# A decoder layer's last FFN piece: its projection put behind the one before it, and its last four tiles multiplied for one half of the tokens at a time

## The chip, the cores and the metric

One core of one Trainium2 chip runs the whole layer in one launch. The metric is the device time of that launch in microseconds (us), and lower is better. Of several executions the median is given.

## The reference, cut to what matters

The kernel computes one decoder layer on 256 tokens of 2048 channels in float32: a token mixer, then a SwiGLU feed-forward network (FFN). Only the end of the FFN matters here.

```python
D_MODEL, SEQ, D_FF = 2048, 256, 5632

def rmsnorm(x, w):
    y = x * lax.rsqrt(jnp.mean(x * x, axis=-1, keepdims=True) + EPS)
    return y * w

def swiglu(h, w_gate_up, w_down):
    gate, up = jnp.split(h @ w_gate_up, 2, axis=-1)
    return (jax.nn.silu(gate) * up) @ w_down

# the last lines of the layer; x is (1, 256, 2048)
h = rmsnorm(x, g_pre_ffn) * (1.0 + sc_f) + sh_f
y = swiglu(h, w_gate_up, w_down)
x = x + ga_f * rmsnorm(y, g_post_ffn)
```

## The kernel before

**Tiles.** A weight tile is 256 rows by 512 columns of a matrix (512 KB). SyncE loads it into a ring of four slots (`RING = 4`), `raw`. ScalarE rounds it to `whi` (`high`), VectorE takes the rest, `raw - whi`, as `wlo` (`low`). TensorE multiplies it in `multiply`: for each half of the tokens (`tt`, 128 rows each) and each 128 rows of the tile three matmuls of 512 columns, so 12 per tile. The activations are split in the same way (`hT_hi` and `hT_lo` for the FFN's input, `oT_hi` and `oT_lo` for its hidden values). Each group of 512 output columns has a pair of PSUM banks, one bank for each half of the tokens. There are two such pairs, used in turn. Banks 4 and 5 (`XA`) take transposes.

**Who waits for whom.** `high(c)` waits until TensorE has finished tile c-4 (semaphore `multiplied`), `low(c)` waits for `high(c)`, TensorE waits for `low(c)` (`lo_ready`), and the load of tile c waits for `low(c-4)`. TensorE starts a group when its pair is free (`pair_free`). Each engine works through its own instructions in program order, and these are written out by hand: at which tile number `c` VectorE adds a finished pair or ScalarE takes a sigmoid stands in the loops over `c`.

**The FFN.** The 5632 hidden channels are 11 pieces of 512 (`NF = 11`, numbered 0 to 10 here). A piece has a gate (8 tiles), an up (8 tiles) and a projection back to 2048 columns (4 groups of 2 tiles). Between up and projection stands a chain: VectorE multiplies the SiLU of the gate by the up (`hidden`), TensorE transposes the product (`transpose_group`, 8 transposes), ScalarE rounds it (`hidden_high`, semaphore `ff_high`) and VectorE takes the rest (`hidden_low`, `ff_low`). To hide it, `channel(n)` runs on TensorE in the order gate of piece n, with the transposes of piece n-1 after its fourth tile, then projection of piece n-1, then up of piece n. VectorE adds the projection's pairs to `ya` with `add_pair`. Piece 10 is the loop `Fori(FF_ADA + 2, NF)` with one turn. Behind it stands the projection of piece 10 alone, at `Place(B_LAST, G_LAST)`, which `hidden_transposed` and the wait for `ff_low` precede.

**The end.** The last projection's four groups are added to `ya` with `add_out`. ScalarE squares and sums each (`square_sum`, for each half of the tokens, in the order of the groups), VectorE multiplies by the gain rows (`gain_out`). Then `reciprocal_rms` sums the squares, GpSimd raises them to the power -0.5 (`power`), and VectorE does `x2 = ya * stat + x2` in eight instructions of 128x512. SyncE stores four blocks of 512 columns, each for all tokens, and waits for the stores.

Of the kernel before, what the change touches and what calls it, by code (L numbers as in the profile page):

```python
# [21 lines left out]
F32 = mybir.dt.float32  # L22
# [8 lines left out]
P = 128  # L31
# [82 lines left out]
def build(nc, x, vectors, consts, masks, positions, ada0, ada1, ada2, ga_bias, post_rows, w_start, w_kr, w_uqn, w_uqr, w_uk, w_uv, w_hf,  # L114
          w_hq, w_hi, w_hg, w_omla, w_ohg, w_out, w_gate, w_up, w_down, out):
    ctx = ExitStack()
    with ctx:
# [13 lines left out]
        oT_hi, oT_lo = cT_hi[:, 0], cT_lo[:, 0]  # L131
        rT_hi, rT_lo = (t[:].rearrange("p a k t -> p (a k) t") for t in (cT_hi, cT_lo))
# [74 lines left out]
        def by_ktile(b):  # L207
            return PS[:, b:b + 2, :].rearrange("p b (k t) -> p (b k) t", t=T)
# [74 lines left out]

        ada_step = sig("ada_step")
# [41 lines left out]
        def _(sp):  # L326
# [102 lines left out]
            with sp.Fori(FF_ADA + 1, NF) as n:  # L429
                load_ff(n, False)  # L430
# [3 lines left out]
            for n in range(GD):  # L434
                sp.wait_ge(sig("x_final"), TT * (n + 1))
                sp.dma_start(out[:, :, n * NW:(n + 1) * NW], x2[:, :, n * NW:(n + 1) * NW])\
                  .then_inc(sig("stored"), 16)
            sp.wait_ge(sig("stored"), 16 * GD)
# [3 lines left out]
        def _(act):  # L442
# [269 lines left out]
            def hidden_high(n):  # L712
                act.wait_ge(sig("ff_transposed"), n)
                nc.scalar.activation(oT_hi, by_ktile(XA), ACT.Copy).then_inc(sig("ff_high"), 1)
# [6 lines left out]
            with act.Fori(1, NF) as n:  # L721
                pl = place_ff(n)
                for c in range(7):
                    high(pl, c)
                hidden_high(n)
                for c in range(7, CD + 3):
                    high(pl, c)
                from_pair(pl, 0, CD - 1, stage[:], ACT.Sigmoid, False, "ff_sigmoid")
                for c in range(CD + 3, F_N):
                    high(pl, c)  # L730
            pl = Place(B_LAST, G_LAST)
            for c in range(RING):
                high(pl, c)
            hidden_high(NF)
            for c in range(RING, GD * CR):
                high(pl, c)
            for n in range(GD):
                p = (G_LAST + n) % 2
                act.wait_ge(pair_free[p], freed_by(p, G_LAST + n + 1))
                for tt in range(TT):  # L740
                    if n or tt:
                        act.wait_ge(sig("y2_squared"), n * TT + tt)
                    square_sum(ya[:, tt, n * NW:(n + 1) * NW], dec[:, 0, 0:NW], sums[:, tt, n:n + 1])\
                        .then_inc(sig("y2_squared"), 1)
# [3 lines left out]
        def _(pool):  # L748
# [27 lines left out]
            power(stat[:, 12:12 + TT], TT, "trunk", 3)  # L776
# [3 lines left out]
        def _(pe):  # L780
# [343 lines left out]
            with pe.Fori(FF_ADA + 2, NF) as n:  # L1124
                channel(n, False)
            pl = Place(B_LAST, G_LAST)
            hidden_transposed(pl)
            pe.wait_ge(sig("ff_low"), NF)
            for j in range(GD):
                multiply(pl, j, CR, j * CR, 0, CR, oT_hi, oT_lo)  # L1130
# [3 lines left out]
        def _(dve):  # L1134
# [478 lines left out]
            def hidden(pl):  # L1613

                dve.wait_ge(multiplied, pl.through(-1))
                p = pl.pair(-1)
                nc.vector.tensor_tensor(stage[:], stage[:], banks(2 * p), ALU.mult).then_inc(pair_free[p], 1)

            def hidden_low(n):
                dve.wait_ge(sig("ff_high"), n)  # L1620
                nc.vector.tensor_tensor(oT_lo, by_ktile(XA), oT_hi.bitcast(F32), ALU.subtract)\
                  .then_inc(sig("ff_low"), 1)
# [46 lines left out]
            with dve.Fori(FF_ADA + 2, NF) as n:  # L1669
                channel(n, False)  # L1670
            pl = Place(B_LAST, G_LAST)

            def add_out(j):

                dve.wait_ge(multiplied, pl.through(j * CR + CR - 1))
                cols = slice(j * NW, (j + 1) * NW)
                p = pl.pair(j)
                nc.vector.tensor_tensor(ya[:, :, cols], ya[:, :, cols], banks(2 * p), ALU.add)\
                  .then_inc(pair_free[p], 1)
                dve.wait_ge(pair_free[p], pl.freed(j) + 1)  # L1680

            def gain_out(j):
# [7 lines left out]
            for c in range(GD * CR):  # L1690
# [108 lines left out]
```

## Time and profile before

| | us |
|---|---|
| median of 3 runs | 1955.16 (1954.36 to 1957.7) |
| the profiled execution, its own time | 1955.46 |
| its span in the profile, first to last instruction | 1953.7 |
| TensorE busy with matmuls | 1846.4 (95%) |
| VectorE busy | 1314.4 (67%) |
| ScalarE busy | 885.0 (45%) |
| GpSimd busy | 109.9 (6%) |

The profile names the engines PE (TensorE matmul), PEld (TensorE weight load), DVE (VectorE), ACT (ScalarE), POOL (GpSimd) and SP (SyncE). L797 is line 797 of the kernel. Times in its rows count from the start of the span. A matmul's duration is that of one instruction from start to end. Since they overlap, the pace is read from start to start. PEclk is the share of TensorE's clock that was granted, 1.00 for 2.4 GHz and 0.50 for 1.2 GHz.

### The profile page before, as it was taken

Reading aid. Unit: us, or ns where it says so; the run is one execution under the profiler, and the core shown is the slowest. Engines: PE = TensorE matmul, PEld = TensorE weight load, DVE = VectorE, ACT = ScalarE, POOL = GpSimd, SP = SyncE. Lnnn points to the kernel's source line nnn. Section 1 sums busy time; section 2 is a strip of 40 time slices with the busy share of each in tenths; the row PEclk is TensorE's granted clock in tenths of the full one; section 3 lists DMA queues with packets and bytes.
Section 4 is the critical chain, followed back from the end, with each engine's and each line's share of the span. In section 5 each row is a group of like instructions: output and inputs, shape, how many; then the busy total and the mean of one; then the engine's idle time right before and its main releaser. Section 6 shows DMA issues by size and latency. Waiting matters only on the chain.

```text
span 1953.7 us, 24693 instructions
## 1 busy us (share of the span) xinstructions
PE 1846.4 (95%) x8884; PEld 1548.0 (79%) x8884; DVE 1314.4 (67%) x1375; ACT 885.0 (45%) x991; POOL 109.9 (6%) x75
## 2 busy tenths in 40 slices
PE   1999999999999999898999996999999999999995
PEld 1877888888888888787888885888888888888884
DVE  5898766678678678666666546566656666665555
ACT  4544455645645644553434443434443444443342
POOL 0000000130130130130000000000000000000000
PEclk9999999999999999999999998999999999999998
DMA  9996546558657657644675652666666666665552
GB/s 382 359 350 242 194 168 224 193 170 284 219 169 270 217 174 258 204 151 152 231 287 203 215 193 86 232 230 208 223 231 227 210 224 224 226 206 177 189 194 76
DMA packets 116497, 423.45 MB, mean 217 GB/s; under 512 B 13008, under 2 KB 13264, under 8 KB 115920
## 3 DMA queue, kind: packets, MB, share of 16 engines
q1 hardware_dynamic: 116432, 422.57, 61.7%
q8 instruction: 42, 0.69, 0.1%
q14 instruction: 23, 0.19, 0.0%
HBM read 420.42 MB, written 2.10 MB: 216 GB/s over the span
## 4 chain that ended last, share of the span: by engine, by line
issue 61%; PE 30%; POOL 4%; DVE 3%; ACT 1%; DMA 1%; SPq 0%; POOLq 0%; DVEq 0%; ACTq 0%
PE PS L797 9%; PE PS L799 9%; PE PS L798 9%; POOL dec L194 2%; DVE ada_acc L1147 1%; POOL dec L195 1%; PE PS L815 1%; DMA zT<-in_ada 1%; DVE wlo L1140 1%; PE PS L939 1%; PE PS L832 1%; PE PS L857 0%; POOL dec L190 0%; ACT whi L449 0%; POOL stat L752 0%
## 5 line engine op out<-in xcount | busy, mean ns | idle before, releaser
L1140 DVE TENSOR_TENSOR wlo<-raw,whi 128x1024 fp32r<-128x1024 f32 x600 | 731.5, 1222 | 464.3 <-ACT whi L449 463.9
L449 ACT ACTIVATE whi<-raw 128x1024 fp32r<-128x1024 f32 x600 | 629.8, 1053 | 758.8 <-PE PS L799 686.9
L797 PE MATMUL PS<-whi,hT_hi 128*128 128x512 f32 x1792 | 710.6, 397 | 13.6 <-DVE wlo L1140 7.6
L799 PE MATMUL PS<-whi,hT_lo 128*128 128x512 f32 x1792 | 700.3, 391 | 0.0
L798 PE MATMUL PS<-wlo,hT_hi 128*128 128x512 f32 x1792 | 700.3, 391 | 0.0
L797 PEld LDWEIGHTS PS<-whi,hT_hi 128*128 128x128 f32 x1792 | 338.4, 189 | 87.5 <-issue 6.2
L799 PEld LDWEIGHTS PS<-whi,hT_lo 128*128 128x128 f32 x1792 | 337.9, 189 | 71.8
L798 PEld LDWEIGHTS PS<-wlo,hT_hi 128*128 128x128 f32 x1792 | 338.4, 189 | 67.5 <-issue 0.2
L797 PE MATMUL PS<-whi,cT_hi 128*128 128x512 f32 (+1 forms) x608 | 239.2, 393 | 9.5 <-DVE wlo L1140 7.1
L799 PE MATMUL PS<-whi,cT_lo 128*128 128x512 f32 (+1 forms) x608 | 236.8, 390 | 0.0
L798 PE MATMUL PS<-wlo,cT_hi 128*128 128x512 f32 (+1 forms) x608 | 236.8, 389 | 0.0
L797 PEld LDWEIGHTS PS<-whi,cT_hi 128*128 128x128 f32 x608 | 116.8, 192 | 33.4 <-DVE wlo L1140 7.8
L799 PEld LDWEIGHTS PS<-whi,cT_lo 128*128 128x128 f32 x608 | 116.3, 191 | 23.5
L798 PEld LDWEIGHTS PS<-wlo,cT_hi 128*128 128x128 f32 x608 | 116.7, 192 | 22.8
L1147 DVE SCALAR_TENSOR_TENSOR ada_acc<-ada_raw,csilu,ada_acc 128x512 f32<-128x512 f32 (+1 forms) x148 | 119.7, 809 | 11.4 <-DMA ada_raw<-in_ada 8.1
L752 POOL TENSOR_TENSOR stat<-stat,con 128x2 f32<-128x2 f32 (+1 forms) x10 | 12.7, 1266 | 1386.3 <-DVE stat L1199 1357.1
L1309 DVE TENSOR_TENSOR gate<-gate,PS 128x1024 f32<-128x1024 f32 x64 | 78.0, 1219 | 14.7 <-PE PS L799 14.6
L194 POOL TENSOR_TENSOR dec<-bT 128x512 f32<-128x512 f32 x28 | 51.5, 1840 | 439.8 <-DVE bT L1397 365.2
L939 PEld LDWEIGHTS PS<-zT 128*128 128x128 f32 x448 | 54.2, 192 | 6.2 <-DVE zT L1416 4.3
L939 PE MATMUL PS<-zT 128*128 128x64 f32 x448 | 53.6, 272 | 3.7 <-DVE zT L1416 3.7
L1429 DVE COPY_PREDICATED pT<-msk,PS 128x512 f32<-128x512 uint8 x28 | 25.1, 896 | 40.2 <-issue 33.4
L578 ACT ACTIVATE dec<-dec 128x1024 f32<-128x1024 f32 (+1 forms) x32 | 32.1, 1004 | 26.3 <-POOL dec L195 26.0
(203 smaller groups left out, 1070.2 us busy)
## 6 DMA issues: line engine op xcount, KB each, us to landing
ada_raw<-in_ada SPq DMA_DIRECT2D x142, 512.0 KB, 4.8
raw<-in_w_gate SPq DMA_DIRECT2D x88, 512.0 KB, 4.3
raw<-in_w_up SPq DMA_DIRECT2D x88, 512.0 KB, 4.3
raw<-in_w_down SPq DMA_DIRECT2D x88, 512.0 KB, 4.3
raw<-in_w_start SPq DMA_DIRECT2D x80, 512.0 KB, 4.4
raw<-in_w_hf SPq DMA_DIRECT2D x32, 512.0 KB, 4.9
raw<-in_w_hq SPq DMA_DIRECT2D x32, 512.0 KB, 5.1
raw<-in_w_hi SPq DMA_DIRECT2D x32, 512.0 KB, 4.1
```

What stands on the lines that cost most here:

```text
L194: eng.tensor_tensor(d[:, :, 1, :], b[:, :, 1, :], end, ALU.subtract)
L195: return eng.tensor_tensor(d[:, :, 0, :], end, b[:, :, 0, :], ALU.subtract)
L449: nc.scalar.activation(whi[:, pl.slot(c), 0:w], raw[:, pl.slot(c), 0:w], ACT.Copy)\
L578: nc.scalar.activation(dif, dif, ACT.Exp).then_inc(sig("decays"), 1)
L797: nc.tensor.matmul(o, hi[:, kt, tok], whi[:, s, cols], start=start, stop=False)
L798: nc.tensor.matmul(o, hi[:, kt, tok], wlo[:, s, cols], start=False, stop=False)
L799: last = nc.tensor.matmul(o, lo[:, kt, tok], whi[:, s, cols], start=False, stop=stop)
L939: last = nc.tensor.matmul(PS[:, XA + L % 4, i * 64:(i + 1) * 64], z[:, i], zt[:, i, :, 1, :], start=True, stop=True)
L1140: nc.vector.tensor_tensor(wlo[:, s, 0:w], raw[:, s, 0:w], whi[:, s, 0:w].bitcast(F32), ALU.subtract)\
L1147: last = nc.vector.scalar_tensor_tensor(out=acc, in0=slot, scalar=csilu[:, a:a + 1], in1=acc, op0=ALU.mult, op1=ALU.add)
L1309: nc.vector.tensor_tensor(dst, dst, banks(2 * p), ALU.add).then_inc(pair_free[p], 1)
L1429: nc.vector.copy_predicated(o, mask.unsqueeze(1).broadcast_to(shape), PS[:, XA + L % 4, :].rearrange("p (i x m) -> p i x m", i=2 * HPG, m=m))\
```

## The change

Pieces 0 to 9 stay as they are, but the projection of piece 9 leaves `channel(10)`, which is written out instead of being a turn of a loop. At `place_end` the order on TensorE is now: gate of piece 10 (tiles 0 to 7, transposes of piece 9 after the fourth), up of piece 10 (`E_UP`, tiles 8 to 15), projection of piece 9 (`E_DOWN`, tiles 16 to 23) with the transposes of piece 10 after its second group, then projection of piece 10 (`E_LAST`, tiles 24 to 31). Its hidden values go to a buffer of their own, `eT_hi` and `eT_lo`. The loads, `high` and `low` follow this order.

Of the last projection the first two groups are multiplied as before. The four tiles of the last two groups stay in the ring together, and TensorE goes through them once for the first half of the tokens and once for the second, six matmuls per tile each time. The end of the kernel then works by halves of the tokens: adds, squares, sum, power, gain and the final `x2` for the first half, then for the second, and SyncE stores 1024 columns of one half at a time.

```diff
+        eT_hi, eT_lo = cT_hi[:, 1], cT_lo[:, 1]
...
+        place_end = Place(B_LAST - F_N, G_LAST - (2 + GD))
+        E_UP, E_DOWN, E_LAST = CD, 2 * CD, F_N
...
-            with sp.Fori(FF_ADA + 1, NF) as n:
-                load_ff(n, False)
+            load_ff(FF_ADA + 1, False)
+            for c in range(E_LAST):
+                if c < E_DOWN:
+                    src = (w_gate, w_up)[c // CD][NF - 1, c % CD]
+                else:
+                    src = w_down[NF - 2, (c - E_DOWN) // CR, (c - E_DOWN) % CR]
+                load(place_end, c, src)
...
-            for n in range(GD):
-                sp.wait_ge(sig("x_final"), TT * (n + 1))
-                sp.dma_start(out[:, :, n * NW:(n + 1) * NW], x2[:, :, n * NW:(n + 1) * NW])\
-                  .then_inc(sig("stored"), 16)
-            sp.wait_ge(sig("stored"), 16 * GD)
+            for tt in range(TT):
+                for h in range(2):
+                    sp.wait_ge(sig("x_final"), tt * GD + 2 * h + 2)
+                    cols = slice(h * 2 * NW, (h + 1) * 2 * NW)
+                    sp.dma_start(out[:, tt, cols], x2[:, tt, cols]).then_inc(sig("stored"), 16)
+            sp.wait_ge(sig("stored"), 16 * TT * 2)
...
-            with act.Fori(1, NF) as n:
+            with act.Fori(1, NF - 1) as n:
...
-            pl = Place(B_LAST, G_LAST)
-            for c in range(RING):
+            pl = place_end
+            for c in range(E_LAST + GD * CR):
                 high(pl, c)
-            hidden_high(NF)
-            for c in range(RING, GD * CR):
-                high(pl, c)
-            for n in range(GD):
-                p = (G_LAST + n) % 2
-                act.wait_ge(pair_free[p], freed_by(p, G_LAST + n + 1))
+                if c == 6:
+                    hidden_high(NF - 1)
+                if c == E_UP + 2:
+                    from_pair(pl, 0, CD - 1, stage[:], ACT.Sigmoid, False, "ff_sigmoid")
+                if c == E_DOWN + 6:
+                    hidden_high(NF, eT_hi)
+
+            def square_last(n, tt):
+                square_sum(ya[:, tt, n * NW:(n + 1) * NW], dec[:, tt, n % 2 * NW:(n % 2 + 1) * NW], sums[:, tt, n:n + 1])\
+                    .then_inc(sig("y2_squared"), 1)
+
+            for n in range(2):
+                p = pl.pair(2 + GD + n)
+                act.wait_ge(pair_free[p], pl.freed(2 + GD + n) + 1)
                 for tt in range(TT):
-                    if n or tt:
-                        act.wait_ge(sig("y2_squared"), n * TT + tt)
-                    square_sum(ya[:, tt, n * NW:(n + 1) * NW], dec[:, 0, 0:NW], sums[:, tt, n:n + 1])\
-                        .then_inc(sig("y2_squared"), 1)
+                    square_last(n, tt)
+            for tt in range(TT):
+                for n in range(2, GD):
+                    act.wait_ge(sig("y2_squared"), 2 * tt + n)
+                    act.wait_ge(sig("y2_added"), tt * 2 + n - 1)
+                    square_last(n, tt)
...
-            power(stat[:, 12:12 + TT], TT, "trunk", 3)
+            for tt in range(TT):
+                power(stat[:, 12 + tt:13 + tt], 1, "trunk", 3 + tt)
...
             with pe.Fori(1, FF_ADA + 1) as n:
                 channel(n, False)
             channel(FF_ADA + 1, True)
-            with pe.Fori(FF_ADA + 2, NF) as n:
-                channel(n, False)
-            pl = Place(B_LAST, G_LAST)
+            pl = place_end
+            multiply(pl, 0, CD, 0, 0, 4, hT_hi, hT_lo)
             hidden_transposed(pl)
+            multiply(pl, 0, CD, 0, 4, CD, hT_hi, hT_lo)
+            multiply(pl, 1, CD, E_UP, 0, CD, hT_hi, hT_lo)
+            pe.wait_ge(sig("ff_low"), NF - 1)
+            for j in range(GD):
+                multiply(pl, 2 + j, CR, E_DOWN + j * CR, 0, CR, oT_hi, oT_lo)
+                if j == 1:
+                    pe.wait_ge(pair_free[pl.pair(1)], pl.freed(1) + 1)
+                    transpose_group(stage, XA).then_inc(sig("ff_transposed"), 1)
             pe.wait_ge(sig("ff_low"), NF)
-            for j in range(GD):
-                multiply(pl, j, CR, j * CR, 0, CR, oT_hi, oT_lo)
+            for j in range(2):
+                multiply(pl, 2 + GD + j, CR, E_LAST + j * CR, 0, CR, eT_hi, eT_lo)
+            for tt in range(TT):
+                for j in range(2, GD):
+                    p = pl.pair(2 + GD + j)
+                    if tt == 0:
+                        pe.wait_ge(pair_free[p], pl.freed(2 + GD + j))
+                    for c in range(CR):
+                        at = E_LAST + j * CR + c
+                        pe.wait_ge(lo_ready, pl.through(at))
+                        s = pl.slot(at)
+                        for k in range(KC):
+                            kt = c * KC + k
+                            tok = slice(tt * P, (tt + 1) * P)
+                            cols = slice(k * NW, (k + 1) * NW)
+                            o = PS[:, 2 * p + tt, :]
+                            nc.tensor.matmul(o, eT_hi[:, kt, tok], whi[:, s, cols], start=c == 0 and k == 0, stop=False)
+                            nc.tensor.matmul(o, eT_hi[:, kt, tok], wlo[:, s, cols], start=False, stop=False)
+                            last = nc.tensor.matmul(o, eT_lo[:, kt, tok], whi[:, s, cols], start=False,
+                                                    stop=c == CR - 1 and k == KC - 1)
+                    last.then_inc(sig("last_rows"), 1)
...
+            def hidden(pl, c=-1, g=-1):
+
+                dve.wait_ge(multiplied, pl.through(c))
+                p = pl.pair(g)
...
             with dve.Fori(1, FF_ADA + 1) as n:
                 channel(n, True)
             channel(FF_ADA + 1, False, True)
-            with dve.Fori(FF_ADA + 2, NF) as n:
-                channel(n, False)
-            pl = Place(B_LAST, G_LAST)
...
+
...
+            def add_rows(j, tt):
+
+                cols = slice(j * NW, (j + 1) * NW)
+                dve.wait_ge(sig("last_rows"), tt * 2 + j - 1)
+                nc.vector.tensor_tensor(ya[:, tt, cols], ya[:, tt, cols], PS[:, 2 * pl.pair(2 + GD + j) + tt, :], ALU.add)\
+                  .then_inc(sig("y2_added"), 1)
...
+            def gain_rows(j, tt):
+
+                cols = slice(j * NW, (j + 1) * NW)
+                nc.vector.tensor_tensor(ya[:, tt, cols], ya[:, tt, cols], post_gain[1][:, cols], ALU.mult)\
+                  .then_inc(sig("y2_gained"), 1)
+
+            for c in range(E_LAST + GD * CR):
                 low(pl, c)
                 if c == 3:
                     hidden(pl)
-                    hidden_low(NF)
-                if c in (4, 6):
-                    add_out((c - 4) // 2)
-            gain_out(0)
-            for j in range(2, GD):
-                add_out(j)
-                gain_out(j - 1)
-
-            dve.wait_ge(sig("y2_squared"), GD * TT)
-            reciprocal_rms(12, 3, lambda: gain_out(GD - 1))
-            for n in range(GD):
-                cols = slice(n * NW, (n + 1) * NW)
-                dve.wait_ge(sig("y2_gained"), n + 1)
-                for tt in range(TT):
+                if c == 6:
+                    hidden_low(NF - 1)
+                if c == E_UP + 3:
+                    silu_gate(pl, NF)
+                if c == E_DOWN + 3:
+                    hidden(pl, E_DOWN - 1, 1)
+                j = c - E_DOWN - CR - 2
+                if j in (0, 2, 4, 6):
+                    j //= 2
+                    add_pair(pl, 2 + j, E_DOWN + j * CR + CR - 1, ya[:, :, j * NW:(j + 1) * NW])
+                if c == E_DOWN + 7:
+                    hidden_low(NF, eT_lo, eT_hi)
+                if c == E_LAST + 4:
+                    add_last(0)
+                if c == E_LAST + 6:
+                    add_last(1)
+            gain_last(0)
+            gain_last(1)
+            for tt in range(TT):
+                for j in range(2, GD):
+                    add_rows(j, tt)
+                dve.wait_ge(sig("y2_squared"), 2 * TT + 2 * tt + 2)
+                nc.vector.tensor_reduce(stat[:, 12 + tt:13 + tt], sums[:, tt], AX.X, ALU.add)\
+                  .then_inc(sig("squares_summed"), 1)
+                dve.wait_ge(sig("squares_summed"), 2 + tt)
+                rsqrt_of(stat[:, 12 + tt:13 + tt], D, "trunk", 3 + tt, lambda: [gain_rows(j, tt) for j in range(2, GD)])
+                for n in range(GD):
+                    cols = slice(n * NW, (n + 1) * NW)
+                    dve.wait_ge(sig("y2_gained"), 2 * (tt + 1) + min(n - 1, 2) if n >= 2 else 2)
                     nc.vector.scalar_tensor_tensor(out=x2[:, tt, cols], in0=ya[:, tt, cols],
                                                    scalar=stat[:, 12 + tt:13 + tt], in1=x2[:, tt, cols],
                                                    op0=ALU.mult, op1=ALU.add).then_inc(sig("x_final"), 1)
```

## Rows read from the trace of the kernel before

**Rows 1.** The page: busy time, share of the span and instructions of each engine.
```profile
PE 1846.4 (95%) x8884; PEld 1548.0 (79%) x8884; DVE 1314.4 (67%) x1375; ACT 885.0 (45%) x991; POOL 109.9 (6%) x75
```

**Rows 2.** Busy time by stretch (start:end, length, engines, PEclk, DMA share, GB/s).
```profile
1855.00:1905.00 50.00, 50.00 (x222) 41.42 (x221) 28.72 (x24) 20.57 (x20) 0.00 (x0) 1.00 0.56 190
...
1915.00:1920.28 5.28, 5.28 (x12) 4.13 (x13) 0.00 (x0) 0.00 (x0) 0.00 (x0) 0.50 0.00 0
```

**Rows 3.** Timeline of TensorE, from the last up tile into the last projection (start, duration).
```profile
1906.67 0.39 PE L799 MATMUL PS<-whi,hT_lo 128*128 128x512 f32 x1
1910.66 1.97 PE L806 MATMUL PS<-con,stage 128*128 128x128 f32 x8 [3.60 <-DVE stage L1617]
1915.00 0.79 PE L797 MATMUL PS<-whi,cT_hi 128*128 128x512 f32 x1 [2.37 <-DVE cT_lo L1621]
...
1923.21 0.39 PE L797 MATMUL PS<-whi,cT_hi 128*128 128x512 f32 x1
...
1928.43 0.39 PE L799 MATMUL PS<-whi,cT_lo 128*128 128x512 f32 x1
...
1939.31 0.39 PE L799 MATMUL PS<-whi,cT_lo 128*128 128x512 f32 x1
```

**Rows 4.** Timeline of TensorE around the transposes of piece 9, inside gate 10.
```profile
1851.61 1.03 PE L806 MATMUL PS<-con,stage 128*128 128x128 f32 x8
...
1853.18 0.39 PE L797 MATMUL PS<-whi,hT_hi 128*128 128x512 f32 x1
```

**Rows 5.** Timeline of ScalarE and VectorE behind the fourth tile of the last projection.
```profile
1928.91 1.06 ACT L449 ACTIVATE whi<-raw 128x1024 fp32r<-128x1024 f32 x1 [1.66 <-PE PS L799]
1929.88 0.61 ACT L460 ACTIVATE dec<-gate 128x512 f32<-128x512 f32 x1
1930.11 1.22 DVE L1140 TENSOR_TENSOR wlo<-raw,whi 128x1024 fp32r<-128x1024 f32 x1
```

**Rows 6.** Timeline from the last add to the end.
```profile
1939.73 1.22 DVE L1678 TENSOR_TENSOR gate<-gate,PS 128x1024 f32<-128x1024 f32 x1 [2.96 <-PE PS L799]
1940.98 0.63 ACT L460 ACTIVATE dec<-gate 128x512 f32<-128x512 f32 x1 [3.96 <-DVE gate L1678]
...
1942.28 0.19 ACT L460 ACTIVATION_READ_ACCUMULATOR dec<-gate 128x1 f32 x1
1942.49 0.16 DVE L1570 TENSOR_REDUCE stat<-sums 128x2 f32<-128x8 f32 x1 [0.28 <-ACT dec L460]
1942.69 0.17 DVE L1199 TENSOR_SCALAR stat<-stat 128x2 f32<-128x2 f32 x1
1942.77 1.22 DVE L1687 TENSOR_TENSOR gate<-gate,mixed 128x1024 f32<-128x1024 f32 x1
1942.94 1.61 POOL L752 TENSOR_TENSOR stat<-stat,con 128x2 f32<-128x2 f32 x1 [755.97 <-DVE stat L1199]
1944.58 5.39 DVE L1708 SCALAR_TENSOR_TENSOR att<-gate,stat,att 128x512 f32<-128x512 f32 x8 [0.59 <-POOL stat L752]
1946.03 4.51 SPq L436 DMA_DIRECT2D out<-att  x4
```

**Rows 7.** Groups of VectorE by shape (busy, mean ns | idle before).
```profile
L1708 DVE SCALAR_TENSOR_TENSOR att<-gate,stat,att 128x512 f32<-128x512 f32 x8 | 5.4, 748 | 0.6 <-POOL stat L752 0.6
...
L1384 DVE TENSOR_TENSOR att<-PS,stat 128x512 f32 x6 | 3.8, 681 | 0.0
```

**Rows 8.** Timeline of GpSimd: two powers in a row, then the memset.
```profile
1175.09 0.70 POOL L752 TENSOR_TENSOR stat<-stat,con 128x2 f32<-128x2 f32 x1 [265.35 <-DVE stat L1199]
1182.81 0.69 POOL L752 TENSOR_TENSOR stat<-stat,con 128x2 f32<-128x2 f32 x1 [7.03 <-DVE stat L1199]
1183.46 3.51 POOL L775 MEMSET gate<- 128x4096 f32 x1
```

**Rows 9.** DMA issues of two stretches: count, KB each, median us to landing.
```profile
out<-att SPq DMA_DIRECT2D x4, 512.0 KB, 3.3
...
raw<-in_w_gate SPq DMA_DIRECT2D x8, 512.0 KB, 4.4
```

More of the change, by code:

```diff
@@ L282, in place_ff @@
             return Place(B_FF1 - F_N, G_FF1 - (2 + GD), F_N, 2 + GD, n)
+        place_end = Place(B_LAST - F_N, G_LAST - (2 + GD))
+        E_UP, E_DOWN, E_LAST = CD, 2 * CD, F_N
+        E_TILES = E_LAST + 2 * CR
         ada_step = sig("ada_step")
@@ L710, in _, with hidden_high @@
                   .then_inc(sig("h2_high"), 1)
-            def hidden_high(n):
+            def hidden_high(n, to=oT_hi):
                 act.wait_ge(sig("ff_transposed"), n)
-                nc.scalar.activation(oT_hi, by_ktile(XA), ACT.Copy).then_inc(sig("ff_high"), 1)
+                nc.scalar.activation(to, by_ktile(XA), ACT.Copy).then_inc(sig("ff_high"), 1)
             for c in range(CD, CD + 3):
@@ L1611, in _, with hidden_low @@
             h2_low(KD // 2 - 1)
-            def hidden(pl):
-                dve.wait_ge(multiplied, pl.through(-1))
-                p = pl.pair(-1)
+            def hidden(pl, c=-1, g=-1):
+                dve.wait_ge(multiplied, pl.through(c))
+                p = pl.pair(g)
                 nc.vector.tensor_tensor(stage[:], stage[:], banks(2 * p), ALU.mult).then_inc(pair_free[p], 1)
-            def hidden_low(n):
+            def hidden_low(n, lo=oT_lo, hi=oT_hi):
                 dve.wait_ge(sig("ff_high"), n)
-                nc.vector.tensor_tensor(oT_lo, by_ktile(XA), oT_hi.bitcast(F32), ALU.subtract)\
+                nc.vector.tensor_tensor(lo, by_ktile(XA), hi.bitcast(F32), ALU.subtract)\
                   .then_inc(sig("ff_low"), 1)
@@ L1668, in _, with add_last, gain_last @@
             channel(FF_ADA + 1, False, True)
-            with dve.Fori(FF_ADA + 2, NF) as n:
-                channel(n, False)
-            pl = Place(B_LAST, G_LAST)
-            def add_out(j):
-                dve.wait_ge(multiplied, pl.through(j * CR + CR - 1))
-                cols = slice(j * NW, (j + 1) * NW)
[L1677 to L1682, printed above, removed]
+            pl = place_end
+            def add_last(j):
+                dve.wait_ge(multiplied, pl.through(E_LAST + j * CR + CR - 1))
+                cols = slice(j * NW, (j + 1) * NW)
+                p = pl.pair(2 + GD + j)
+                nc.vector.tensor_tensor(ya[:, :, cols], ya[:, :, cols], banks(2 * p), ALU.add).then_inc(pair_free[p], 1)
+                dve.wait_ge(pair_free[p], pl.freed(2 + GD + j) + 1)
+            def add_rows(j, tt):
[3 more added lines that the diff above has]
+                  .then_inc(sig("y2_added"), 1)
+            def gain_last(j):
                 cols = slice(j * NW, (j + 1) * NW)
@@ L1688, in gain_out @@
                                         .broadcast_to([P, TT, NW]), ALU.mult).then_inc(sig("y2_gained"), 1)
-            for c in range(GD * CR):
+            def gain_rows(j, tt):
[3 more added lines that the diff above has]
+            for c in range(E_LAST + GD * CR):
                 low(pl, c)
```

## The prediction

> **What bounds the kernel now.** I read the page first. TensorE is busy for 95% of the span [rows 1], so work shortens the kernel only where TensorE waits, runs slowly, or has finished. Next the busy time by stretch: with the FFN in full flow it is busy 50.00 of 50.00 us at a granted clock of 1.00 [rows 2]. Nothing that hides there behind TensorE has a price. Then the timeline of the last 50 us, engine by engine, which shows two exceptions.
>
> The first is the last projection's chain. The last up matmul starts at 1906.67 and the projection's first at 1915.00 [rows 3]. In between stand VectorE's product, eight transposes, ScalarE's rounding and VectorE's rest, one after the other. The clock is at 0.50 (1.2 GHz) in the next 5.28 us [rows 2].
>
> The second is the end. The last matmul starts at 1939.31 [rows 3] and the last add at 1939.73. Squares, sum, power and eight final instructions follow, up to 1944.58 + 5.39 = 1949.97 [rows 6]. The span ends at 1953.7. The last store lands some 3.3 us after its issue [rows 9].
>
> **Term 1: TensorE's stream.** Before, from the last up matmul to the last of all is 1939.31 - 1906.67 = 32.64 us. At full clock matmuls stand (1939.31 - 1923.21) / 71 = 0.2268 us apart [rows 3], so 96 of them need 21.77 us. The other 10.87 us are idle time (1915.00 - 1906.90 = 8.10) and the half clock (1923.21 - 1915.00 = 8.21 for 24 matmuls that need 5.44, so 2.77).
>
> After, the same tiles are multiplied, and the transposes of piece 10 stand in a running stream. What such transposes cost is seen in gate 10: they start at 1851.61, and the fourth matmul behind them at 1853.18 [rows 4], so the first would at full pace stand at 1853.18 - 3 x 0.2268 = 1852.50. That is 0.89 us. Term 1 is 10.87 - 0.89 = **9.98 us**, if nothing new waits.
>
> So I walk through the new order. ScalarE starts `high` 0.48 us behind a tile's last matmul (1928.91 against 1928.43) and takes 1.06 [rows 3, 5]. `low` takes 1.22 [rows 5], so a tile is ready 2.8 us after the tile four places earlier ended. A tile lasts 12 x 0.2268 = 2.72 us.
> - Let U be the start of the last up matmul. `hidden` for piece 10 stands behind `low(19)` and is done at U + 4. TensorE wants its pair for the second group at U + 5.4 and the transposes at U + 10.9: margins of 1.4 and 7 us.
> - The transposes end near U + 12. `hidden_high(NF, eT_hi)` waits for them on ScalarE, and `high(23)` is queued behind it, so tile 23 is ready at about U + 15.3. It is wanted at U + 20.0. `hidden_low(NF)` follows at U + 16.5, and is wanted at U + 22.9, a margin of 6 us. The load of tile 27, queued behind `low(23)`, lands some 4.4 us later [rows 9], at U + 20, and `high(27)` can't start before U + 23.
> - Let M be the start of the last matmul of tile 27, the last before the four tiles that are gone through twice. In the first pass a tile lasts 1.36 us. `low(31)` stands behind `add_last(1)` on VectorE, which can start at M + 0.42 (1939.73 against 1939.31 [rows 3, 6]). It is done at M + 1.68 + 1.22 = M + 2.90, and TensorE wants it after 18 more matmuls, M + 4.31. The pair of the fourth group is free at M + 1.64, wanted at M + 2.95. These margins of 1.3 to 1.4 us are the narrowest.
>
> The gate and up of piece 10 follow each other as the up of one piece and the gate of the next do now. The loads, their number and sizes are those of before in another order. Loop or written out, TensorE's stream holds the same instructions. I take 0 for these, since there is no wait to see [rows 2].
>
> **Term 2: the end.** Before, the last final instruction ends 1949.97 - 1939.31 = 10.66 us behind the last matmul's start. After, the last matmul starts at M + 48 x 0.2268 = M + 10.88, and I follow ScalarE and VectorE from M.
> - ScalarE: `high(31)` from M + 0.48. The first four squares start 0.97 us later (1929.88 against 1928.91 [rows 5]) and come every 0.74 us (two take 1942.28 + 0.19 - 1940.98 = 1.49 [rows 6]). They end at M + 4.4.
> - VectorE: two gains of 1024 columns (1.22 each [rows 6]) behind these squares, done at M + 5.6. Then the two adds of the first half. A 512-column add out of PSUM took 0.681 elsewhere [rows 7], and one starts some 0.62 after the other. They end at M + 6.24 and M + 6.84. Their groups were ready at M + 3.1 and M + 5.9.
> - ScalarE squares both by M + 7.76. VectorE sums at M + 7.78, scales at M + 7.98. From scaling to GpSimd is 0.25, the power 1.61, to VectorE 0.03 [rows 6], so M + 9.87. Its two gains (1.3 us) lie under the power. Four final instructions follow that take 0.75 each, at a pace of (5.39 - 0.75) / 7 = 0.663 [rows 6, 7]. They end at M + 12.61.
> - The second half was ready at M + 8.6 and M + 11.3, but is queued behind them: adds from M + 12.53 to M + 13.83, squares by M + 14.73, scaling at M + 14.95. Here the power follows another power. Such a one took 0.69, against 1.61 behind the memset [rows 6, 8]. Then the two gains bind, not the power: M + 14.95 + 0.08 + 0.62 + 0.68 = M + 16.33. The four final ones end at M + 19.09.
>
> That is 19.09 - 10.88 = 8.21 us behind the last matmul's start, **2.45 us** less. Bounds: with 1.61 for the second power the end is 0.49 later, and with 0.69 for the first, 0.49 earlier. The gains then bind in both halves. I take 1.61 and 0.69, since what ran before each is as in the rows. The last store is 512 KB as before. Its lines are 4 KB instead of two of 2 KB, which the trace shows only for loads. They land in 4.4 us beside other transfers, the stores in 3.3 [rows 9]. So 0 to 1.1 us more, and I take 0, because little else moves then.
>
> The Trainium skill ("GPSIMD Engine Reference", section 2.1, Instruction dispatch) puts a dispatch at tens of cycles for each instruction and makes no difference by what ran before. By that rule alone both powers cost the same, and the gain would be 12.0 instead of 12.4. The rows show the difference [rows 6, 8].
>
> **Sum.** 9.98 + 2.45 = 12.4 us. The profiled execution took 1955.46, so 1943.0; it stood 0.3 above the median, so **1942.7 us** against 1955.16.
>
> **The rivals.**
> - *Only the stall goes.* Halving the last groups makes VectorE's queue longer: four final instructions of the first half stand in front of the second half's adds, 1.2 us after those were ready (M + 12.5 against M + 11.3). If the small instructions, their semaphores or the stores cost more than in my walk, term 2 falls to nothing and the gain is 9.98: 1945.2. Against it: nearly all durations are in the rows.
> - *A new wait takes part of it.* If `low(31)` or the fourth pair comes more than 1.3 us late, or `hidden_high` holds `high(23)` back by over 4.7 us, TensorE waits within the last projection. A wait of 3 us with a lower clock behind it for a few tiles costs about 5 to 6 us: 1948. Up to 8.5 us of loss it is still faster by over 0.2%.
> - *Slower: the clock falls and stays down.* At 0.50 the 12 matmuls of a tile took 5.28 us [rows 2] instead of 2.72, so 2.6 us more. If a wait before the transposes of piece 10 throws the clock down and it stays down for the last 12 tiles, that is 31 us, and the time 1942.7 + 31 = 1974. It decides from 12.4 / 2.6 = 4.8 tiles on. For it: after the stall now the clock was at 0.50 for 5.28 us [rows 2]. Against it: it came back within two tiles, the margins there are over 4 us, and the clock is at 1.00 across the same transposes in gate 10, where the pace is full again by the fourth matmul [rows 4].
> - *The change doesn't do what it says* would be transposes that wait for `hidden` after all. With a margin of 7 us I give that no chance of its own.
>
> **How the numbers follow.** A measurement of this kernel can tell about 0.2%, 3.9 us, from no change. Chances: both terms as worked out, a gain of 11 to 14 us, 0.77. Only the stall goes, 8.5 to 11 us, 0.13. A new wait takes part, 0 to 8.5 us, 0.08, of which half leaves under 3.9. Slower by over 0.2%, 0.02. Faster is then 0.94, the same 0.04, slower 0.02. The likeliest case reaches from 1941.2 to 1944.2. The range takes in the bounds of power and store, the case without term 2, and the spread of three runs (3.3 us): 1940.5 to 1946.7.
>
> **What the changed profile would show.** No wait of TensorE at the transposes of piece 10, which stand in the running stream with 0.8 to 0.9 us from first to next matmul. A clock of 1.00 in the last projection. The last matmul starts near 1929.3. GpSimd's two powers take 1.6 and 0.7 us. The last final instruction ends near 1937.5, and the span at 1941.3. The prediction is wrong if TensorE waits in front of `low(31)`, if its clock drops, or if the distance from the last matmul to the end of the span isn't shorter by 2 to 3 us.

## The result

| | before | after |
|---|---|---|
| median, us | 1955.13 (4 runs, 1954.36 to 1957.70) | 1943.01 (4 runs, 1940.24 to 1944.19) |
| profiled execution: its own time, span | 1955.46, 1953.7 | 1944.19, 1942.4 |

The ratio is 0.993 (95% interval 0.9917 to 0.9942), so the kernel is faster by 0.58 to 0.83%. The median fell by 12.1 us, and 12.4 was forecast. The terms behind that number were less exact than the number, as both traces show. They are measured from the start of the span over three points to its end: the transposes in gate 9 (a piece that is the same in both kernels), the last matmul's start, and the end of the last final instruction.

| us | before | after | difference | forecast |
|---|---|---|---|---|
| start of the span to the transposes in gate 9 | 1785.44 | 1788.47 | +3.03 | 0 |
| from there to the last matmul's start | 153.87 | 143.89 | -9.98 | -9.98 |
| from there to the end of the last final instruction | 10.66 | 6.98 | -3.68 | -2.45 |
| from there to the end of the span | 3.73 | 3.06 | -0.67 | 0 |

The transposes in gate 9, in TensorE's timeline of before and of after:

```profile
1785.44 1.03 PE L806 MATMUL PS<-con,stage 128*128 128x128 f32 x8
...
1788.47 1.03 PE L828 MATMUL PS<-con,stage 128*128 128x128 f32 x8
```

TensorE's timeline in the kernel after, where [rows 3] stood. Its `multiply` is now at L819 to L821, the transposes at L828, and the split groups at L1174 to L1176.

```profile
1887.94 0.39 PE L821 MATMUL PS<-whi,hT_lo 128*128 128x512 f32 x1
...
1899.06 1.03 PE L828 MATMUL PS<-con,stage 128*128 128x128 f32 x8
1899.85 0.48 PE L819 MATMUL PS<-whi,cT_hi 128*128 128x512 f32 x1
...
1921.48 0.39 PE L821 MATMUL PS<-whi,cT_lo 128*128 128x512 f32 x1
...
1932.36 0.39 PE L1176 MATMUL PS<-whi,cT_lo 128*128 128x512 f32 x1
```

The transposes of piece 10 stand in a running stream, with 0.79 us to the next matmul and no idle time in brackets. The busy time by stretch from the last up tile to the last matmul, against [rows 2]: TensorE is busy in all of the 45.60 us, and the granted clock is 1.00.

```profile
1887.00:1932.60 45.60, 45.60 (x206) 37.62 (x205) 33.53 (x34) 18.57 (x26) 0.93 (x1) 1.00 0.40 125
```

The end of the kernel after, from its timeline, against [rows 6]: VectorE from its first two gains on, with GpSimd's two powers and the stores.

```profile
1924.30 2.44 DVE L1739 TENSOR_TENSOR gate<-gate,mixed 128x1024 f32<-128x1024 f32 x2
...
1926.65 1.38 DVE L1731 TENSOR_TENSOR gate<-gate,PS 128x512 f32<-128x512 f32 x2
...
1929.08 0.15 DVE L1247 TENSOR_SCALAR stat<-stat 128x1 f32<-128x1 f32 x1
1929.15 1.28 DVE L1745 TENSOR_TENSOR gate<-gate,mixed 128x512 f32<-128x512 f32 x2
1929.31 0.93 POOL L773 TENSOR_TENSOR stat<-stat,con 128x1 f32<-128x1 f32 x1 [740.56 <-DVE stat L1247]
1930.35 2.73 DVE L1781 SCALAR_TENSOR_TENSOR att<-gate,stat,att 128x512 f32<-128x512 f32 x4
1931.79 7.92 SPq L448 DMA_DIRECT2D out<-att  x4
1933.00 1.28 DVE L1731 TENSOR_TENSOR gate<-gate,PS 128x512 f32<-128x512 f32 x2
...
1935.34 0.15 DVE L1247 TENSOR_SCALAR stat<-stat 128x1 f32<-128x1 f32 x1
1935.41 1.28 DVE L1745 TENSOR_TENSOR gate<-gate,mixed 128x512 f32<-128x512 f32 x2
1935.57 0.93 POOL L773 TENSOR_TENSOR stat<-stat,con 128x1 f32<-128x1 f32 x1 [5.33 <-DVE stat L1247]
1936.61 2.73 DVE L1781 SCALAR_TENSOR_TENSOR att<-gate,stat,att 128x512 f32<-128x512 f32 x4
```

Both powers take 0.93 us, where I had 1.61 and 0.69. Neither power decides: the first ends at 1929.31 + 0.93 = 1930.24, the two gains beside it at 1929.15 + 1.28 = 1930.43, and in the second half the same gap of 0.19 us stands between them. The four final instructions of the first half start at 1930.35, as VectorE's second gain comes to its end, which is M + 8.9 instead of M + 9.9 (M = 1921.48). The last ends at 1936.61 + 2.73 = 1939.34.

### The profile page after: what moved, and what is told of

Its sections match the earlier page's. It is cut to its first block, busy times and chain, and to the rows that moved or that the text cites. A ratio compares the mean times of both kernels' runs of the same rounds, so it can differ in the third digit from the quotient of the medians.

```text
span 1942.4 us, 24551 instructions
## 1 busy us (share of the span) xinstructions
PE 1844.0 (95%) x8884; PEld 1547.6 (80%) x8884; DVE 1315.0 (68%) x1381; ACT 884.6 (46%) x991; POOL 110.3 (6%) x76
## 4 chain that ended last, share of the span: by engine, by line
PE 66%; issue 23%; DVE 4%; POOL 4%; ACT 1%; DMA 1%; SPq 0%; DVEq 0%; POOLq 0%; ACTq 0%
PE PS L819 21%; PE PS L821 21%; PE PS L820 20%; POOL dec L195 2%; DVE ada_acc L1195 2%; POOL dec L196 1%; PE PS L837 1%; PE PS L828 1%; DVE wlo L1188 1%; DMA zT<-in_ada 1%; PE PS L961 1%; PE PS L854 1%; PE PS L1110 1%; ACT whi L460 0%; PE PS L879 0%
## 5 line engine op out<-in xcount | busy, mean ns | idle before, releaser
L819 PE MATMUL PS<-whi,hT_hi 128*128 128x512 f32 x1792 | 711.4, 397 | 15.1 <-DVE wlo L1188 9.2
L821 PE MATMUL PS<-whi,hT_lo 128*128 128x512 f32 x1792 | 701.4, 391 | 0.0
L819 PEld LDWEIGHTS PS<-whi,hT_hi 128*128 128x128 f32 x1792 | 338.9, 189 | 88.6 <-issue 6.2
L821 PEld LDWEIGHTS PS<-whi,hT_lo 128*128 128x128 f32 x1792 | 338.3, 189 | 72.1
L819 PE MATMUL PS<-whi,cT_hi 128*128 128x512 f32 (+1 forms) x592 | 231.1, 390 | 7.1 <-DVE wlo L1188 7.1
L820 PE MATMUL PS<-wlo,cT_hi 128*128 128x512 f32 (+1 forms) x592 | 229.0, 387 | 0.0
L821 PE MATMUL PS<-whi,cT_lo 128*128 128x512 f32 (+1 forms) x592 | 229.0, 387 | 0.0
L819 PEld LDWEIGHTS PS<-whi,cT_hi 128*128 128x128 f32 x592 | 112.6, 190 | 29.6 <-DVE wlo L1188 7.9
L821 PEld LDWEIGHTS PS<-whi,cT_lo 128*128 128x128 f32 x592 | 112.4, 190 | 22.5
L820 PEld LDWEIGHTS PS<-wlo,cT_hi 128*128 128x128 f32 x592 | 112.6, 190 | 21.7
L773 POOL TENSOR_TENSOR stat<-stat,con 128x2 f32<-128x2 f32 (+2 forms) x11 | 12.9, 1176 | 1376.8 <-DVE stat L1247 1347.5
```

The costliest lines, as they stand in the source:

```text
L819: nc.tensor.matmul(o, hi[:, kt, tok], whi[:, s, cols], start=start, stop=False)
L820: nc.tensor.matmul(o, hi[:, kt, tok], wlo[:, s, cols], start=False, stop=False)
L821: last = nc.tensor.matmul(o, lo[:, kt, tok], whi[:, s, cols], start=False, stop=stop)
```

## The experiments

Four things were open: whether the two halves of the change act apart, what sets the power's duration, why the stores land sooner, and whether the 3.0 us at the start belong to the change.

**1. The order alone** (`e1_order`). The changed kernel's order of pieces, with the end of the kernel before.

```diff
             pe.wait_ge(sig("ff_low"), NF)
-            for j in range(2):
+            for j in range(GD):
                 multiply(pl, 2 + GD + j, CR, E_LAST + j * CR, 0, CR, eT_hi, eT_lo)
-            for tt in range(TT):
...
+            dve.wait_ge(sig("y2_squared"), GD * TT)
+            reciprocal_rms(12, 3, lambda: gain_last(GD - 1))
```

> The new order of the pieces alone, with the end of the kernel as it was before. Theory: the order gives 9.98 us of TensorE's stream, so from the transposes in gate 9 to the last matmul it takes 143.9 us instead of 153.9, the clock stays at 1.00 in the last projection, and from the last matmul to the end of the span it takes 14.4 us as before. Time 1945 +- 2. Rival (most of the gain is the end's, and the order gives little): 153.9 us stay above 147, time 1950 or more. On the other point, the whole kernel's start: in the changed kernel the transposes in gate 9 came 3.0 us later than before. If that is the change's doing (code written out), they come near 1788.5 here too; if it differs from execution to execution, they can stand anywhere between 1783 and 1790.

Measured: 1946.87 us against 1955.69 for the kernel before on the same chip, ratio 0.9957 (0.9941 to 0.9974). From the transposes in gate 9 to the last matmul it takes 143.89 us, and 14.38 from there to the end of the span. In the trace the order gives its 9.98 us and leaves the end as it was. The medians differ by 8.8 us.

**2. The halves alone** (`e2_halves`). The kernel before, with the changed kernel's last two groups and end.

```diff
-            for j in range(GD):
+            for j in range(2):
                 multiply(pl, j, CR, j * CR, 0, CR, oT_hi, oT_lo)
+            for tt in range(TT):
+                for j in range(2, GD):
...
+                    last.then_inc(sig("last_rows"), 1)
```

> The end by halves of the tokens alone, with the old order of the pieces. Theory: the stall in front of the last projection stays (8.1 us idle, then 1.2 GHz), and from the last matmul to the end of the span it takes 10.0 us instead of 14.4, as in the changed kernel. Time 1955.1 - 4.4 = 1950.8. Rival (what I forecast, 2.45 us from the last matmul to the last final instruction and nothing at the stores): 11.9 us, time 1952.7. Rival that the halves only gain where TensorE has run at 2.4 GHz all along: less than 2 us.

Measured: 1951.80 against 1955.69, ratio 0.9977 (0.9968 to 0.9987). From the last matmul to the end of the span it takes 10.06 us, as in the changed kernel, and the stall is there. The two parts of the change add up: 8.8 and 3.9 us by the medians, against 12.1 for both. The stall cost less this time: 152.73 us instead of 153.87 to the last matmul. Why it varies is told under term 1.

**3. The power with nothing beside it** (`e3_power_alone`), and **4. a power in front of it** (`e4_power_before`). Both start from the kernel before.

```diff
 e3_power_alone
-            reciprocal_rms(12, 3, lambda: gain_out(GD - 1))
+            reciprocal_rms(12, 3)
+            gain_out(GD - 1)
 e4_power_before
+            pool.wait_ge(sig("sums_zeroed"), 1)
+            nc.gpsimd.tensor_tensor(stat[:, 14:14 + TT], con[:, K_ONE:K_ONE + TT], con[:, K_POW:K_POW + TT], ALU.pow).then_inc(sig("spare_power"), 1)
             power(stat[:, 12:12 + TT], TT, "trunk", 3)
```

> The kernel before, with the last gain of 1024 columns behind the wait for the power instead of beside it. Theory A (a power takes 0.7 us behind another power and 1.6 behind anything else, as I forecast): it still stands behind the memset, so 1.6 us, and the last final instruction ends 1.2 us later than before, 11.9 us behind the last matmul. Theory B (GpSimd is held up while VectorE's gain runs beside it): 0.7 us, and the last final instruction ends 0.3 us later than before, 11.0 us.

> The kernel before, with one more power on two spare columns right behind the memset, so that the last power stands behind a power. The gain stays beside it. Theory A (what ran before on GpSimd sets its duration): 0.7 us, and the finals start when the gain ends, about 0.6 us sooner. Theory B (VectorE's gain beside it holds it up): 1.6 us as before.

The timeline of VectorE and GpSimd in `e3_power_alone`:

```profile
1943.19 0.70 POOL L752 TENSOR_TENSOR stat<-stat,con 128x2 f32<-128x2 f32 x1 [755.88 <-DVE stat L1199]
1943.93 1.23 DVE L1687 TENSOR_TENSOR gate<-gate,mixed 128x1024 f32<-128x1024 f32 x1 [0.81 <-POOL stat L752]
```

And in `e4_power_before`:

```profile
1185.05 3.51 POOL L775 MEMSET gate<- 128x4096 f32 x1
...
1188.62 1.21 DVE L1142 TENSOR_TENSOR wlo<-raw,whi 128x1024 fp32r<-128x1024 f32 x1
1188.64 1.75 POOL L777 TENSOR_TENSOR stat<-con 128x2 f32<-128x2 f32 x1
...
1944.24 1.22 DVE L1689 TENSOR_TENSOR gate<-gate,mixed 128x1024 f32<-128x1024 f32 x1
1944.41 1.61 POOL L752 TENSOR_TENSOR stat<-stat,con 128x2 f32<-128x2 f32 x1 [754.03 <-DVE stat L1201]
```

The same power behind the memset takes 0.70 us when the gain comes after it, and behind another power still 1.61 when the gain runs beside it. So the power waits for the gain, and the theory with which I forecast falls. The gain runs from 1944.24 to 1945.46, and the power ends 0.56 us after it. The spare power in the same trace is a second case: it started 0.02 us after one of VectorE's `low` instructions of 1024 columns, took 1.75 us, and also ended 0.56 us after it (1190.39 against 1189.83). The Trainium skill says so ("SBUF — State Buffer", section Who interferes with whom): a VectorE instruction with two inputs in SBUF contends with a GpSimd instruction that reads SBUF. The trace agrees with 1.61 against 0.70 us. I had not drawn on it. In the changed kernel the gains beside the power are 512 columns, and it took 0.93 us, between the two. It is also one column wide instead of two there, and which of the two differences counts for how much wasn't tried. Leaving the gain beside the power is still right: in `e3_power_alone` the last final instruction ended 10.89 us behind the last matmul, instead of 10.66.

**5. The stores** (`e5_stores`). The kernel before, with final instructions and stores in the order of the halves.

```diff
-            for n in range(GD):
-                sp.wait_ge(sig("x_final"), TT * (n + 1))
-                sp.dma_start(out[:, :, n * NW:(n + 1) * NW], x2[:, :, n * NW:(n + 1) * NW])\
+            for tt in range(TT):
+                for h in range(2):
+                    sp.wait_ge(sig("x_final"), tt * GD + 2 * h + 2)
+                    cols = slice(h * 2 * NW, (h + 1) * 2 * NW)
+                    sp.dma_start(out[:, tt, cols], x2[:, tt, cols]).then_inc(sig("stored"), 16)
```

> The kernel before, with its eight final instructions in the order of the token halves and stores of 1024 columns of one half: lines of 4 KB instead of two of 2 KB. Theory: the line length makes a store land in 2.6 us instead of 3.3, and the span ends 3.1 us behind the last final instruction instead of 3.7; nothing else moves. Rival (in the changed kernel the stores land sooner because the pairs of stores come in two bursts with a gap between them): here, with all four in a row, 3.3 and 3.7 us stay.

Its DMA issues near the end, against [rows 9]:

```profile
out<-att SPq DMA_DIRECT2D x4, 512.0 KB, 2.7
```

All four stores follow each other as before, and they land in 2.7 us instead of 3.3. The span ends 3.02 us behind the last final instruction instead of 3.73. So it is the shape of the stores, not the gap between them. Longer lines are also fewer lines (128 for a store instead of 256), and these two weren't tried apart. The one run took 1954.13 us.

**6. Late transposes** (`e7_late`). The changed kernel, with the transposes of piece 10 behind the whole projection of piece 9. `hidden_low(NF, eT_lo, eT_hi)` moves from `E_DOWN + 7` to `E_LAST + 2`.

```diff
-                if c == E_DOWN + 6:
+                if c == E_LAST + 2:
                     hidden_high(NF, eT_hi)
...
-                if j == 1:
+                if j == 3:
                     pe.wait_ge(pair_free[pl.pair(1)], pl.freed(1) + 1)
                     transpose_group(stage, XA).then_inc(sig("ff_transposed"), 1)
```

> The changed kernel with the transposes of piece 10 behind all four groups of the projection of piece 9 instead of behind two. Theory (the stream hides the chain of transposes, rounding and rest, and nothing else): TensorE waits for that chain only, 0.48 + 1.03 + 1.22 us and some, about 3 us behind the transposes, less than the 8.1 of before because product and transposes are not waited for. From the transposes in gate 9 to the last matmul 147 to 149.5 us instead of 143.9, depending on whether the clock drops. Rival (the gain came from something else in the new order, such as the loads): 144 us.

TensorE's timeline in `e7_late`:

```profile
1910.96 1.03 PE L828 MATMUL PS<-con,stage 128*128 128x128 f32 x8
1914.37 0.50 PE L819 MATMUL PS<-whi,cT_hi 128*128 128x512 f32 x1 [2.37 <-DVE cT_lo L1669]
```

The wait is back, 2.37 us long, in front of the last projection. From the transposes in gate 9 to the last matmul it takes 148.19 us, 4.30 more than in the changed kernel. The first four matmuls behind the wait run at full pace, and then the clock falls.

```profile
1914.30:1915.40 1.10, 1.03 (x4) 0.86 (x5) 1.10 (x2) 0.00 (x0) 0.00 (x0) 1.00 0.00 0
1915.40:1920.50 5.10, 5.10 (x17) 4.00 (x16) 0.52 (x2) 1.06 (x1) 0.00 (x0) 0.67 0.28 103
```

In these two stretches the granted clock is 1.00 and then 0.67 in the mean. In the second one eight matmuls in a row stand 0.42 to 0.43 us apart, and then they follow each other every 0.23 us again. So with the last part of the chain uncovered, 4.30 of the 9.98 us are lost again, and even a wait of 2.4 us was followed by a stretch at half clock. The product and the wait for it stayed covered here. One run took 1949.48 us.

**7. The start.** In the first profiles the four kernels with the new order reached the power in front of the FFN at 1184.6 to 1186.3, and the five with the old one at 1182.8 to 1184.4. Up to there they hold the same instructions. That looked like an effect of the code written out. I ran the kernel before with its last turn written out on four engines (`e8_written_out`), the kernel before again, and the changed kernel twice.

```diff
-            with act.Fori(1, NF) as n:
+            def channel_high(n):
...
+            with act.Fori(1, NF - 1) as n:
+                channel_high(n)
+            channel_high(NF - 1)
...
-            with pe.Fori(FF_ADA + 2, NF) as n:
-                channel(n, False)
+            channel(FF_ADA + 2, False)
```

> The kernel before, with the last turn of its FFN loops written out on all four engines, and order and end as they were. What is open is the start of the kernel: in the four kernels with the new order GpSimd's power before the FFN started at 1184.6 to 1186.3, in the five with the old order at 1182.8 to 1184.4, with the same instructions up to there. Theory (chance: each execution differs by up to 3 us there): it can fall anywhere from 1182.5 to 1186.5, and the time equals that of before within 1 us. Rival (writing out the last turn on ScalarE and SyncE, which moves the code, costs some 1.5 us further up): 1184.5 or more, and a time 1 to 2 us above that of before. In both the gain at the end is nil: 153.9 us from the transposes in gate 9 to the last matmul, and 14.4 us behind it.

> The kernel before once more, for the start alone. Theory (chance): the power before the FFN anywhere from 1182.5 to 1186.5. Rival (it is the program's doing): below 1184.5.

> The changed kernel once more. Theory (chance): the power before the FFN anywhere from 1182.5 to 1186.5; the end takes 143.9 and 10.0 us as before. With a start like that of before the time should be 14.3 us lower, 1941.4. Rival (it is the program's doing): 1184.5 or more, and a time 12 to 13 us lower.

> The changed kernel a third time, for the start alone. Chance: anywhere from 1182.5 to 1186.5. Rival: 1184.5 or more.

Measured: `e8_written_out` 1956.23 against 1955.97, ratio 1.0001 (0.9991 to 1.001). `r1_before` 1955.03. `r2_after` 1942.90 against 1955.97, ratio 0.9936 (0.9922 to 0.9949). `r3_after` 1942.61. GpSimd's timeline in `r2_after`:

```profile
1181.20 0.69 POOL L773 TENSOR_TENSOR stat<-stat,con 128x2 f32<-128x2 f32 x1 [7.03 <-DVE stat L1247]
```

That is the earliest of all thirteen profiles, in the kernel whose first profile had 1184.59. `r3_after` had 1183.66, so two profiles of the changed kernel stand below the 1184.5 that the rival asked for. The others were 1184.52 in `e8_written_out` and 1182.41 in `r1_before`. My own bounds, 1182.5 to 1186.5, were too narrow on the low side. The same program differs by 3.4 us there, and by 4.65 us at the transposes in gate 9 (1783.82 in `r2_after` against 1788.47). So the 3.03 us lie within what chance does. Writing the turn out costs nothing that the time shows, but the interval, about 2 us either way, is too wide to exclude a cost of 1 to 2 us by itself. What differs between executions up to that point wasn't traced further.

**8. A woven end** (`e6_woven`). Once the durations were known, the second half's adds seemed to be queued behind the first half's final instructions for no reason.

```diff
+            add_rows(2, 0)
+            add_rows(3, 0)
+            summed(0, lambda: [gain_rows(2, 0), gain_rows(3, 0)])
+            add_rows(2, 1)
+            for n in range(3):
+                final(n, 0)
+            add_rows(3, 1)
+            dve.wait_ge(sig("y2_squared"), 3 * TT + 1)
+            gain_rows(2, 1)
+            summed(1, lambda: [gain_rows(3, 1), final(3, 0)])
+            for n in range(GD):
+                final(n, 1)
```

> The changed kernel with the adds of the second half, one of its gains and the last final instruction of the first half woven together: add (2,1) before the first half's finals, add (3,1) before its last one, that one beside the second power. Theory (behind the last matmul VectorE's queue is what counts): the last final instruction ends 6.3 us behind the last matmul's start instead of 7.0, and the time is 0.7 us lower, 1942.3, which a ratio can't tell. Rival (the chain add, square, sum, power, finals of the last group binds, not the queue): 7.0 us stay.

VectorE's timeline in it:

```profile
1932.05 0.68 DVE L1731 TENSOR_TENSOR gate<-gate,PS 128x512 f32<-128x512 f32 x1
...
1934.44 3.40 DVE L1782 SCALAR_TENSOR_TENSOR att<-gate,stat,att 128x512 f32<-128x512 f32 x5
```

The last matmul starts at 1931.47 and the last final instruction ends at 1934.44 + 3.40 = 1937.84, 6.37 us later instead of 6.98. The time is 1942.67 against 1955.97 for the kernel before, ratio 0.9931 (0.9918 to 0.9945). Against 1942.90 for the changed kernel in another session this can't be told from no change. Only the trace shows the 0.6 us.

## Why the prediction was right, point by point

**What bounds the kernel: right.** The stream of TensorE and the end behind it were the two places. The order alone and the halves alone gave their parts one by one.

**Term 1, 9.98 us: right to 0.01 us in the two traces**, 153.87 against 143.89. The walk through the new order held too. `hidden_low(NF)` ended at 1904.50, U + 16.56 with U = 1887.94, where I had U + 16.5, and TensorE didn't wait:

```profile
1903.28 1.22 DVE L1669 TENSOR_TENSOR cT_lo<-PS,cT_hi 128x1024 fp32r<-128x1024 f32 x1
```

But 9.98 is one draw. In the seven profiles with the old order the same distance was 152.38 to 153.87 us (mean 153.3), and in the five with the new order and its transposes where the change puts them always 143.88 or 143.89. The wait itself varies little. What varies is where the clock falls and where it comes back. In `r1_before` (152.68) the transposes still ran at full pace, 1.09 us for the eight instead of 1.97 [rows 3]:

```profile
1911.40 1.09 PE L806 MATMUL PS<-con,stage 128*128 128x128 f32 x8 [3.60 <-DVE stage L1617]
1914.87 0.79 PE L797 MATMUL PS<-whi,cT_hi 128*128 128x512 f32 x1 [2.37 <-DVE cT_lo L1621]
```

From the transposes to the next matmul it took 3.47 us instead of 4.34, which is 0.87 of the 1.19 us by which `r1_before` is shorter. The rest is that the full pace was back sooner: over the seven profiles, 10 to 13 of the projection's first matmuls were slow. So term 1 is 8.5 to 10.0 us, 9.4 in the mean, and that the one trace of before stood at the upper end was luck for the match of 0.01 us.

**Term 2, 2.45 us: the way of working was right, the size and one mechanism in it wrong.** It measured 4.35 (3.68 up to the last final instruction, 0.67 at the stores).
- The power. I took 1.61 and 0.69 from what ran before it, and experiments 3 and 4 show that it is what runs beside it. All six powers of 128x2 in the trace of before fit both theories, so the rows couldn't choose. With the shorter gains both took 0.93, so they cost the same, as in the prediction's other case, though not 1.61. And at 0.93 the gains bind in both halves, which the prediction had only as a bound. (By its own walk the gains would end at 7.98 + 0.08 + 0.62 + 0.68 = 9.36, so that bound is 9.87 - 9.36 = 0.51 us, not 0.49, and 1.61 for the second power leaves a gain of 11.9, not 12.0.) From scaling to the first half's final instructions it took 1930.35 - 1929.08 = 1.27 us instead of 1.89.
- The first four squares came every 0.61 us instead of 0.74, as the lines below show. I had taken the pace from a row in which each waits for the one before it ([rows 6]). In the change they have a buffer of their own each and don't wait. Both were changed at once, and neither was tried alone. Scaling came at 1929.08, M + 7.6 instead of M + 8.0.
- The two together put the second half's adds at M + 11.5 instead of M + 12.5, and its own chain took 6.3 us instead of 6.6. That is 1.23 us of the 1.90 by which the term was too small.
- The stores. I took 0 and gave 0 to 1.1 us more as the bound. It was 0.67 less, and `e5_stores` alone gave 0.71 (3.02 instead of 3.73). The loads in [rows 9] that I bounded it by run beside other traffic, so their 4.4 us said nothing of the length of a line. My range had no gain there, and nothing excluded one.

ScalarE's timeline in the kernel after, the first four squares:

```profile
1922.93 0.61 ACT L471 ACTIVATE dec<-gate 128x512 f32<-128x512 f32 x1
...
1923.54 0.62 ACT L471 ACTIVATE dec<-gate 128x512 f32<-128x512 f32 x1
...
1924.16 0.62 ACT L471 ACTIVATE dec<-gate 128x512 f32<-128x512 f32 x1
...
1924.77 0.62 ACT L471 ACTIVATE dec<-gate 128x512 f32<-128x512 f32 x1
```

**The sum** came out at 12.4 against a measured 12.1 by luck. Term 2 was 1.90 us too small, and in this pairing the changed kernel started late. By the traces the change is worth 9.4 + 4.35 = 13.8 us. The starts, which differ by chance from execution to execution, hid a part of it in the first pairing (3.03 us in the profiled executions). In the second pairing, that of `r2_after`, the medians differ by 13.1 us, where I had expected 14.3 for equal starts. The interval of either ratio holds 12.4 and 13.8.

**What the profile should show.** The transposes, the clock and a stream without waits came as written. Four numbers did not: the powers took 0.93 us each instead of 1.6 and 0.7, the last matmul started at 1932.36 instead of 1929.3 (the 3.03 us of the start), the last final instruction ended at 1939.34 instead of 1937.5, and the span at 1942.4 instead of 1941.3. And one of the prediction's own signs of being wrong stands: the distance from the last matmul to the end of the span should have become shorter by 2 to 3 us, and it became shorter by 4.35. The gain of 12.1 us lies in the case "both terms as worked out", but one of the two wasn't.

**The rivals.** That only the stall goes is excluded by `e2_halves`. A new wait: none is in the trace, and `e7_late` shows what it takes, moving the transposes by two groups. The clock that falls and stays: it didn't fall. `e7_late` shows that it falls after a wait of 2.4 us, but comes back, and the whole costs 4.3 us, less than half of what the order gives.

## What to carry to other kernels

Where a chain of small steps on other engines stands between two blocks of matmuls, look for independent matmuls to put in between. It returned the wait and the half clock behind it, and one trace of before gave its size to 1.5 us, since the clock's part of it varies between executions. For the end behind the last matmul, price each small instruction from a row in the same company: a power of two columns took 0.70 or 1.61 us by what VectorE did beside it, and squares came every 0.61 us, or every 0.74 where each waits for the one before. Where a difference of spans and a sum of terms disagree, measure both traces from a common point, since the same program differed by 4.65 us before it reached the part that was changed.

## What the runs showed of the hardware

- A power of 128x2 on GpSimd took 0.70 us alone and 1.61 beside a VectorE product of 1024 columns out of SBUF. It ended 0.56 us after that product, and so did another one, of 1.75 us, beside a VectorE subtraction of 1024 columns (`e4_power_before`). What GpSimd ran before it made no difference.
- Stores of 512 KB in lines of 4 KB landed in 2.6 to 2.7 us, in two lines of 2 KB for each partition in 3.3.
- With the same two waits the granted clock fell at different points, before the transposes or behind them, and came back after 10 to 13 slow matmuls. That made 1.5 us between profiles of the old order. In `e7_late`, with one wait of 2.37 us, it fell four matmuls after TensorE had started again.
